# Compressed attention scores with the operands' sides swapped, and the next group's queries finished earlier

## The reference

```python
s_c = jnp.einsum('bqgrd,bcgd->bgrqc', qb, k_cmp) * scale + dense_bias(t[:, None] - cmp_end[None, :])
p_c = masked_softmax(s_c, valid_c) * jnp.any(valid_c, axis=-1)[:, None].astype(jnp.float32)
o_c = jnp.einsum('bgrqc,bcgd->bqgrd', p_c.astype(v_cmp.dtype), v_cmp)
```

## Time and profile before

| what | value |
|---|---|
| median of 3 runs | 2561.86 us (2561.2 to 2564.33) |
| profiled execution, its own time | 2556.7 us |
| its span | 2554.9 us |
| busy: TensorE, its weight loads, VectorE, ScalarE, GpSimd | 2460.6, 2055.1, 1412.0, 962.9, 173.1 us |
| mean granted TensorE clock | 0.982 |

### The profile page before, as it was taken

One profiled execution on the slowest core, in us unless ns is written; L12 is line 12 of the kernel. 1 busy time (PEld: TensorE's weight loads), 2 busy tenths in 40 slices (PEclk: granted clock), 3 DMA queues, 4 the chain that ended last, 5 costly groups with the idle time before them and its releaser, 6 DMA issues.

```text
span 2554.9 us, 31373 instructions
## 1 busy us (share of the span) xinstructions
PE 2460.6 (96%) x12046; PEld 2055.1 (80%) x12046; DVE 1412.0 (55%) x2965; ACT 962.9 (38%) x1784; POOL 173.1 (7%) x236
## 2 busy tenths in 40 slices
PE   7999999999999999989999999999998997999997
PEld 6888888888887878778888888878876886788886
DVE  5435555676567566765443446666543566543444
ACT  4323334432344444553322334655422345322321
POOL 0000000100001111220000000222100002000000
PEclk9999999999999999999999999999998999899998
DMA  3454433333321111103223224211121341223222
GB/s 131 119 123 128 111 110 137 102 105 112 103 75 62 50 58 67 46 28 113 99 88 102 99 88 138 68 51 58 56 77 66 116 140 50 79 88 106 99 85 89
DMA packets 86093, 231.36 MB, mean 91 GB/s; under 512 B 8456, under 2 KB 23432, under 8 KB 85946
## 3 DMA queue, kind: packets, MB, share of 16 engines
q1 hardware_dynamic: 78480, 217.18, 26.1%
q10 hardware_dynamic: 7466, 12.19, 2.4%
HBM read 217.79 MB, written 11.53 MB: 90 GB/s over the span
## 4 chain that ended last, share of the span: by engine, by line
PE 87%; DVE 7%; ACT 3%; issue 2%; POOL 1%; ACTq 0%; DMA 0%; SPq 0%; DVEq 0%
PE bank L912 86%; PE bank L1082 1%; DVE t_pp L1943 1%; DVE t_PS L1739 1%; POOL t_pw L2327 1%; ACT t_pp L1492 1%; DVE t_wlo L1734 1%; ACT t_PS L1372 0%; ACT t_whi L1372 0%; DVE t_tmp L1783 0%; DVE t_QS L2036 0%; DMA t_raw<-in_f_in 0%; ACT t_XH L1372 0%; PE bank L1253 0%; ACT t_tmp L1372 0%
## 5 line engine op out<-in xcount | busy, mean ns | idle before, releaser
L912 PE MATMUL bank<-t_XH,t_whi 128*128 128x512 f32 x2064 | 819.0, 397 | 22.9 <-DVE t_XL L1743 19.6
L912 PE MATMUL bank<-t_XL,t_whi 128*128 128x512 f32 x2064 | 808.8, 392 | 0.0
L912 PE MATMUL bank<-t_XH,t_wlo 128*128 128x512 f32 x2064 | 808.6, 392 | 0.0
L1734 DVE TENSOR_TENSOR t_wlo<-t_raw,t_whi 128x1024 fp32r<-128x1024 f32 (+2 forms) x420 | 481.7, 1148 | 417.0 <-ACT t_whi L1372 413.9
L1372 ACT ACTIVATE t_whi<-t_raw 128x1024 fp32r<-128x1024 f32 (+2 forms) x420 | 415.5, 991 | 453.3 <-PE bank L912 406.5
L912 PEld LDWEIGHTS bank<-t_XH,t_whi 128*128 128x128 f32 x2064 | 391.0, 189 | 107.7 <-issue 15.0
L912 PEld LDWEIGHTS bank<-t_XH,t_wlo 128*128 128x128 f32 x2064 | 390.7, 189 | 83.5
L912 PEld LDWEIGHTS bank<-t_XL,t_whi 128*128 128x128 f32 x2064 | 391.2, 190 | 78.1
L912 PE MATMUL bank<-t_RX,t_whi 128*128 128x512 f32 x1056 | 325.0, 389 | 0.0
L1813 DVE TENSOR_TENSOR t_tmp<-bank,t_RB 128x512 f32<-128x512 f32 x178 | 122.5, 688 | 233.6 <-PE bank L912 231.3
L912 PEld LDWEIGHTS bank<-t_RX,t_whi 128*128 128x128 f32 x1056 | 198.2, 188 | 41.2
(11 more groups left out here) (305 smaller groups left out, 2752.4 us busy)
## 6 DMA issues: line engine op xcount, KB each, us to landing
t_raw<-in_f_in SPq DMA_DIRECT2D x88, 512.0 KB, 3.2
t_raw<-in_f_out SPq DMA_DIRECT2D x32, 384.0 KB, 3.1
t_raw<-in_w_conv SPq DMA_DIRECT2D x24, 512.0 KB, 3.2
t_raw<-in_w_merge SPq DMA_DIRECT2D x24, 512.0 KB, 3.2
t_raw<-in_fg SPq DMA_DIRECT2D x22, 512.0 KB, 3.2
t_raw<-in_fu SPq DMA_DIRECT2D x22, 512.0 KB, 3.2
t_raw<-in_f_out SPq DMA_DIRECT2D x32, 320.0 KB, 2.8
t_raw<-in_w_g SPq DMA_DIRECT2D x16, 512.0 KB, 3.2
```

Source lines behind the costliest of these rows:

```text
L912: return e.matmul(o, l, r, start=start, stop=stop, skip_group_check=True)
L1734: e.tensor_tensor(wlo[n % NRAW][:, 0:width], raw[n % NRAW][:, 0:width], f32(whi[n % NHI][:, 0:width]), ALU.subtract).then_inc(*w_lo.tick(n))
```

## The change

The scores are made with the sides swapped: the keys of a group are the stationary operand and the queries move, 512 columns at a time. For each head r a stationary tile of 128 columns holds the 32 keys in columns 32r to 32r + 31 and zeros elsewhere, so that the four heads add up in one bank, each on its own 32 partitions. The pair `PCT` is borrowed for these tiles: GpSimd clears it (`cclear`), ScalarE copies the keys in. After eight matmuls ScalarE copies the bank to `T[4]`, four transposes (`cback`) turn it back, and `csoft` reads that bank, now with one add for all four heads. The steps move to other query tiles, and the next group's job is finished before tile 2 of head (3, 0).

```diff
-SMALL = dict(..., cscore=16, cturn=2, ...
+SMALL = dict(..., cscore=8, cback=2, cturn=2, ...
...
-            small = {(1, 0): {0: one("cscore", g), 1: one("csoft", g, 0), 2: one("csoft", g, 1), 3: one("csoft", g, 2)},
-                     (1, 1): {0: one("csoft", g, 3), 1: one("cnorm", g, 0), 2: one("cnorm", g, 1), 3: one("cnorm", g, 2)},
-                     (2, 0): {0: one("cnorm", g, 3), 2: one("cturn", g)}}
+            small = {(1, 0): {0: one("cclear", g), 2: one("cscore", g), 3: one("cback", g)},
+                     (1, 1): {0: one("csoft", g, 0), 1: one("csoft", g, 1), 2: one("csoft", g, 2), 3: one("csoft", g, 3)},
+                     (2, 0): {0: one("cnorm", g, 0), 1: one("cnorm", g, 1), 2: one("cnorm", g, 2), 3: one("cnorm", g, 3)},
+                     (2, 1): {1: one("cturn", g)}}
...
+                    if g < 3 and (r, a) == (3, 0):
+                        at[2] = lambda g=g: w.finish(own[g + 1], jobs)
...
         def cscore(g):
-            b = take("tp", ("cscore", g), True)
+            b = take("tp", ("cscore", g))
             operand(("sq", g, 1))
-            operand(("kc",))
+            operand(("kcp", g))
+            for r in range(4):
+                for q in range(2):
+                    f = mm(b, PCT[q][:, r * P:(r + 1) * P], QS[g % 2][:, r, :], r == 0 and q == 0, r == 3 and q == 1)
+            f.then_inc(*full.tick(("cscore", g)))
+
+        def cback(g):
+            b = take("tp", ("cback", g), True)
+            on.wait_ge(*copied.at(("ct", g)))
             for i in range(4):
-                n = 8 * i + 8
-                for r in range(4):
...
-            f.then_inc(*full.tick(("cscore", g)))
+                f = e.transpose(b[:, i * P:(i + 1) * P], T[4][:, i * P:(i + 1) * P], ident)
+            f.then_inc(*full.tick(("cback", g)))
...
+        def cclear(g):
+
+            on.wait_ge(*x_lo.at(("kc",)))
+            on.wait_ge(*cleared.at(("kcp", g)))
+            for q in range(2):
+                o = bass.AP(PCT[q].tensor, PCT[q].offset, [list(PCT[q].ap[0]), [160, 4], [1, 32]])
+                copy(o, f32(KC[q][:, g * 32:g * 32 + 32]).unsqueeze(1).to_broadcast([P, 4, 32])).then_inc(*x_hi.tick(("kcp", g)))
+
+        def cscore(g):
+            on.wait_ge(*full.at(("cscore", g)))
+            if g:
+                on.wait_ge(*calc.at(("merged", 0, 2 * g - 1, 3)))
+            copy(T[4], banks[("cscore", g)]).then_inc(*copied.tick(("ct", g), ("free", ("cscore", g))))
...
-            for r in range(4):
-                e.tensor_tensor(sc[:, r, :], ps[:, r, :], TB[r][:, c0:c0 + 16 * (n - 1) + 1:16], ALU.add).then_inc(
-                    *evac.tick(("cs", g, i), ("free", ("cscore", g))))
+            e.tensor_tensor(sc, ps, TB4[:, :, c0:c0 + 16 * (n - 1) + 1:16], ALU.add).then_inc(
+                    *evac.tick(("cs", g, i), ("free", ("cback", g))))
...
+        def cclear(g):
+            on.wait_ge(*full.at(("values", 3 + 8 * g)))
+            for q in range(2):
+                e.memset(f32(PCT[q]), 0.0).then_inc(*cleared.tick(("kcp", g)))
```

More of the change, by code:

```diff
@@ L184 @@
 WIDE = dict(wide=24, memv=12, cmp=7, sv=13, mk2=13, mv2=13)
-SMALL = dict(widestat=2, widefin=2, sqstat=4, sqfin=4, skstat=4, skfin=4, cscore=16, cturn=2, hturn=1, kc1=2, vc=1, gn=2,
+SMALL = dict(widestat=2, widefin=2, sqstat=4, sqfin=4, skstat=4, skfin=4, cscore=8, cback=2, cturn=2, hturn=1, kc1=2, vc=1, gn=2,
              gdec=8, gvt=2, gkt=2, gcum=5, gnorm=2, gspread=2, nstat=2, nspread=2, mk2s=1)
@@ L768, in build @@
     KQ = [place(f"KQ{q}", 25216 + q * P, P) for q in range(4)]
-    TB = [place(f"TB{r}", 3072 + 512 * r, 512) for r in range(4)]
+    TB4 = place("TB", 3072, 2048).rearrange("p (r n) -> p r n", r=4)
+    TB = [TB4[:, r, :] for r in range(4)]
     VS = place("VS", 5120, 5120, F32R).rearrange("p (a c j n) -> p a c j n", a=2, c=2, j=4)
@@ L1359, in pe_program @@
                   turn=turn, values=values, rel=rel, kvc=kvc, cmp=cmp, hturn=hturn, kc1=kc1, kc2=kc2, vc=vc, ng=ng, gn=gnt, sq=sq,
-                  sqstat=sqstat, sqfin=sqfin, sk=sk, skstat=skstat, skfin=skfin, sv=sv, cscore=cscore, cnorm=cnorm, cturn=cturn,
+                  sqstat=sqstat, sqfin=sqfin, sk=sk, skstat=skstat, skfin=skfin, sv=sv, cscore=cscore, cback=cback, cnorm=cnorm, cturn=cturn,
                   sgate=sgate, po=po, ka=ka, va=va, vas=vas, qa=qa, gout=gout, gateu=gateu, alr=alr, gkt=gkt, gvt=gvt,
@@ L1715, in act_program @@
                   gateu=gateu, weigh=weigh, turn=turn, rel=rel, table_out=table_out, cmp=cmp, kc1=kc1, kc2=kc2, vc=vc, ng=ng, sq=sq,
-                  sqfin=sqfin, sk=sk, skfin=skfin, skput=skput, svs=svs, csoft=csoft, cturn=cturn,
+                  sqfin=sqfin, sk=sk, skfin=skfin, skput=skput, svs=svs, cclear=cclear, cscore=cscore, csoft=csoft, cturn=cturn,
                   msplit=msplit, winzero=winzero, kaz=kaz, vas=vas, qa=qa, oa=oa, om=om, gdec=gdec, gexp=gexp, gln=gln, gcum=gcum, gvt=gvt,
@@ L2087, in csoft @@
             if i == 0:
-                on.wait_ge(*full.at(("cscore", g)))
+                on.wait_ge(*full.at(("cback", g)))
                 for r in range(4):
                     on.wait_ge(*d_tb[r].at(g))
-                if g:
-                    on.wait_ge(*added(0, 2 * g - 1))
             c0 = 415 - 128 * i
-            ps = banks[("cscore", g)][:, i * P:(i + 1) * P].rearrange("p (r c) -> p r c", r=4)[:, :, 0:n]
-            for r in range(4):
-                e.tensor_tensor(sc[:, r, :], ps[:, r, :], TB[r][:, c0:c0 + 16 * (n - 1) + 1:16], ALU.add).then_inc(
-                    *evac.tick(("cs", g, i), ("free", ("cscore", g))))
+            ps = banks[("cback", g)][:, i * P:(i + 1) * P].rearrange("p (r c) -> p r c", r=4)[:, :, 0:n]
+            e.tensor_tensor(sc, ps, TB4[:, :, c0:c0 + 16 * (n - 1) + 1:16], ALU.add).then_inc(
+                    *evac.tick(("cs", g, i), ("free", ("cback", g))))
             on.wait_ge(*evac.at(("cs", g, i)))
@@ L2340, in sparsezero @@
             e.memset(PC, 0.0).then_inc(*cleared.tick("sparse"))
-        do = dict(scale=scale, hidzero=hidzero, sparsezero=sparsezero)
+        def cclear(g):
+            on.wait_ge(*full.at(("values", 3 + 8 * g)))
+            for q in range(2):
+                e.memset(f32(PCT[q]), 0.0).then_inc(*cleared.tick(("kcp", g)))
+        do = dict(cclear=cclear, scale=scale, hidzero=hidzero, sparsezero=sparsezero)
         for (kind, *args), _ in w.items:
```

6 lines of the change are left out of this document (1 added, 5 removed).

## The result

| | before | changed |
|---|---|---|
| median of runs, on the same chip | 2561.53 us (4 runs, 2559.25 to 2564.33) | 2547.12 us (4 runs, 2545.55 to 2548.81) |
| ratio, 95% interval | | 0.9943, 0.9926 to 0.9961 |
| span of the profiled execution | 2554.9 us | 2545.5 us |
| mean granted TensorE clock | 0.982 | 0.985 |

The changed kernel is 14.4 us faster; 8.3 us were forecast. Over all executions whose clock is on record, 40 of the kernel before and 14 of the changed one, the means are 2558.9 and 2548.4 us, 10.5 us apart.

A forecast was written before the change was run, and what follows sets the result against it. TensorE bounds the kernel (87% of the chain), level with VectorE in group 3. Group gains 3.2 + 4.3 + 0 + 2.1 less 1.3 of waits give 8.3 us, from 2561.9 to 2553.5 us; range 2544 to 2563.

The forecast's parts named there:

- What survives: Sparse branch by groups: 3.2, 4.3, 0 and 2.1 us kept in groups 0 to 3, less 1.3 of waits, 8.3 us faster.
- Scores: Compressed scores on TensorE: 3.57 us of narrow matmuls replaced by 1.84 plus 0.60 of transposes, net 1.13 us a group.
- Clock: Dense work behind the four score sets: 31.0 us at low clock regained at 45%, 3.1 us a group, 4.6 in group 1.
- the clock falls all the same: Rival, behind the new scores: the 31 us at low clock stay; 2 us faster, 2560 us; chance 0.12.
- Bias adds: VectorE's four bias adds per query tile become one over all heads: 1.8 us to 0.9, saving 0.9 us a group.
- New steps: Clearing on GpSimd (1.1 us) and ScalarE copies per group make TensorE wait 1.3 us in all, between 0 and 4.
- the new chain shows: Rival: six handovers from clearing to add cost 1.5 us more a group, 6 of the 8.3 us lost, 2559.5; chance 0.14.
- Moved work: Early finish takes two dense units, 11.1 us of cover, from group 2; VectorE 82% busy there, so its 4.2 us are eaten.
- near 67: Sign that the forecast is right: group 2 takes near 67 us, expected 67.4 (78.5 - 11.1).
- group 2 gain 0: Group 2: all 4.2 us from clock and scores counted as eaten, since VectorE is 82% busy without the moved units.
- The slower rival: Group 2 stays 78.5 us though 11.1 us of cover left it: 7.6 us slower, 2569.5; chance 0.10.
- full return: Rival: VectorE had waited for TensorE during low clock, so idle stretches shrink too; about 16 us faster, 2546; chance 0.22.

## Why the prediction was right, and where it was off

The mechanism was right: wide scores keep the clock up, and this gives the larger part of the gain. The forecast of 8.3 us lies under all three measurements of the gain (14.4, 11.0, 9.5), and the step that was too small is "What survives".

**Scores.** Forecast 1.13 us less a group, measured 1.26 (the transposes occupy 0.38 us by their starts, not the 0.60 of the earlier trace rows). Right.

**Clock.** The cause was right and is shown: no fall behind wide scores in the changed kernel, none behind 128 columns in the kernel before. The rival "the clock falls all the same" is out, and with it the rule of the Trainium skill (TensorE: Matmul & The Clock Gate, HAM oscillation) as the only cause: it names idle gaps, and the trace disagrees for these sets, which had no gap and few columns. The forecast was 31.0 us less at the low level and the trace shows 30.6 of them gone; 6.6 us more elsewhere were not forecast, so net 24.0. What low clock the changed kernel has left, 20.4 us, lies beside TensorE's waits, 6.8 us of it beside the wait of 4.1 us in group 2. Over the whole program the mean granted clocks of all executions say much the same. Worked out from them, the kernel before spends about 103 us at the low level (mean of 40 executions) and the changed one 81 (mean of 14), 22 less.

**Bias adds.** Forecast 0.9 us saved a group. The adds of the four query tiles now take 0.19 to 0.36 us, with a median of 0.28 about 1.1 in all against 1.8: 0.7. The price of about 0.25 each was near.

**New steps.** Clearing 0.53 and key copies 0.31 us came as priced. TensorE's waits were forecast at 1.3 us in all and are 1.5 + 1.4 = 2.9. The size was off since the bank copy was taken as covered: it shows in all four groups, 0.2 to 0.8 us each. The rival "the new chain shows" was right that the chain shows, at 1.6 us over the count instead of its 6; the experiment with more clearing says that it has no room to grow in groups 0 and 3.

**Moved work.** Held. From group 2's scores to group 3's, the stretch of the earlier trace rows, and then a piece of 25 us in it:

```profile
1006.60:1075.20 68.60, 59.42 (x358) 50.07 (x358) 51.23 (x189) 41.40 (x119) 19.83 (x33) 0.93 0.11 37
...
1020.00:1045.00 25.00, 17.77 (x104) 14.43 (x104) 20.06 (x75) 14.51 (x38) 5.34 (x9) 0.80 0.06 19
```

The stretch took 68.6 us, against "near 67". The 70 matmuls fewer than before (428) are 20 of the scores and two dense units, 48, but for two. In the bare piece VectorE is busy 80%, forecast 82%, and TensorE idles 7.2 us of 25, behind the waits of 4.1 and 2.7 us shown above. So "group 2 gain 0" had the right reason; it came out 1.3 us longer for the same work (78.4 - 68.6 = 9.8 shorter, with 11.1 moved out). The fall behind the narrow set is gone there too, but the falls beside the two waits take as much: 10.2 us of low clock before, 10.2 after. The slower rival wanted over 76.0 us there and is out.

**What survives.** This is the step that was mis-sized. The groups, with group 0 counted from the branch's first scores, against the forecast of 3.2, 4.3, 0 and 2.1 less 1.3 for the waits:

| group | before | changed, three executions | gain, with the moved unit put back |
|---|---|---|---|
| 0 | 121.5 | 116.6, 116.6, 116.6 | 4.9 |
| 1 | 129.1 | 128.7, 128.8, 129.1 | 5.8 |
| 2 | 90.0 | 85.6, 85.6, 87.4 | -1.8 |
| 3 | 59.9 | 56.5, 56.5, 56.5 | 3.4 |

The sum is 12.3 us with the waits already in it, where the forecast had 8.3. The factors "three quarters" and "half" for groups 0, 1 and 3 were too small: they feared that VectorE and ScalarE would turn the time that TensorE saves into waiting. TensorE's idle time there changed by only -0.8, +0.9 and +0.5 us. That it changed so little because VectorE had itself waited for TensorE during the low clock is the view of the rival "full return", and is argued, not shown. The agreement of single groups with their 4.2, 5.7 and 4.2 us is in part luck: low time fell by 3.4 us in group 0 and by 10.2 in group 3, not by the 6.9 of the forecast in each.

The rival "full return" was nearer in groups 0, 1 and 3, but its 16 us are above all three measurements, and its own sign failed: it wanted VectorE idle less than 15% in group 2 with the group near 63 us, and VectorE is idle 25% of 68.6 us.

**What no step held.** The profiled execution is 9.4 us shorter in span, though its branch ended 14.2 us earlier. The prediction costed nothing behind the branch. Between the two lie 4.8 us. They go with more low clock behind the branch, and the last section shows why that may be luck: the traced execution of the kernel before took 2556.7 us at a clock of 0.982, which only one of its 40 others reached.

## What to carry to other kernels

A set of narrow matmuls can be paid twice, as these 32 of 8 to 32 columns were: once for itself, 3.57 us, and again by the dense work behind it, 6.9 to 10.3 us at half the clock. Compare the spacing of the same dense matmul before and after such a set, and read the granted clock there. Before restructuring, widen the columns alone with the same instructions; if the time falls, the clock was the cost. A wait that vanishes when a step is moved later has to be looked for at the engine's next in-order step before it is called a gain. And before two traces are compared over a whole program, compare a stretch that has the same instructions in both: here 3570 equal matmuls differed by 1.2 us.

## What was not expected of the hardware

Equal gaps of TensorE bring the clock down in one place and not in another. At the merge behind the branch, TensorE waits 2.20 us in both kernels, then does the same matmuls. Before, and then changed:

```profile
1146.38 0.70 PE L912 MATMUL bank<-t_MG,t_whi 128*128 128x512 f32 x2 [2.20 <-DVE t_MG L1743]
1146.92 0.39 PE L912 MATMUL bank<-t_MG,t_wlo 128*128 128x512 f32 x1
```

```profile
1132.18 0.83 PE L916 MATMUL bank<-t_MG,t_whi 128*128 128x512 f32 x2 [2.20 <-DVE t_MG L1764]
1132.81 0.63 PE L916 MATMUL bank<-t_MG,t_wlo 128*128 128x512 f32 x1
```

and the windows of TensorE's busy time and clock behind it, 1146:1150 before and 1132:1136 after:

```profile
1146.00:1150.00 4.00, 3.62 (x16) 1.00 0.59 184
```

```profile
1132.00:1136.00 4.00, 3.82 (x10) 0.57 0.72 212
```

One matmul takes 0.39 us at 1.00 and 0.63 at the low level. It could be taken for an effect of the change, but the other traces don't bear that out. Of the three traces of the changed kernel the clock fell here in two and stayed up in the third. Over all 13 traces it fell in 6 and stayed up in 7, the wait being 2.2 us in each. And one execution shows both: the kernel before waits 2.04 us in front of `t_OA` at 1889.38, 1904.06 and 1918.74. The clock stays up behind the first two and falls behind the last. The windows behind the second and the third:

```profile
1904.00:1908.00 4.00, 3.94 (x17) 1.00 0.02 6
1919.00:1923.00 4.00, 4.00 (x12) 0.57 0.00 0
```

What makes the difference between equal gaps, these runs don't show.

It matters for reading a gain. Behind the branch the changed kernel's profiled execution spends 57.9 us at the low level, the one before 45.0; 12.9 x 0.45 = 5.8 us, against the 4.8 us by which the rest of the program is longer (1416.4 against 1411.6). The two other executions of the changed kernel spend 57.5 and 54.1 us there, and the version with the transposes two tiles later 48.3. So in these traces the later falls took back a third of the branch's gain. But the kernel before was traced once, and by its granted clock that execution had about 92 us at the low level, where the mean of its 40 others is 103. Over all executions the changed kernel has 22 us less at the low level, nearly all of the 24.0 that its branch alone saved in the trace. That the change itself brings the clock down behind the branch is therefore not shown, and the averages speak against it.
